# Sample pairs inside the attention, and an out-projection that begins while its last norm group is summed

## What is computed

```
z = rmsnorm(x) @ w_in                     # split among the three mixers
out_a = RG-LRU(z)                         # 256 wide
out_b = MLA(z)                            # 8 heads x 64 = 512 wide
out_c = GLA(z)                            # 4 heads x 64 = 256 wide, normed and gated
merged = concat(rmsnorm(out_a, n_a), rmsnorm(out_b, n_b), rmsnorm(out_c, n_c))
x = x + merged @ w_out                    # 1024 x 1024
x = x + hier_moe(rmsnorm(x))              # best of 4 groups, 2 of its 8 experts
```

## Time and profile before

| | before |
|---|---|
| median of 3 runs | 1611.6 us (1609.57 to 1612.38) |
| the profiled execution | 1611.4 us, its span 1609.5 us |
| mean granted TensorE clock | 0.888 of full speed |
| TensorE busy | 1275.7 us, 79% of the span |
| TensorE weight loads | 767.7 us, 48% |
| VectorE busy | 545.7 us, 34% |
| ScalarE busy | 359.1 us, 22% |
| GpSimd busy | 320.8 us, 20% |
| chain of waits, by engine | PE 52%, DMA 22%, DVE 11%, waits for nothing shown 6%, SyncE's queue 4% |

### The profile page before, as it was taken

One profiled execution on the slowest core, in us unless ns is written; L12 is line 12 of the kernel. 1 busy time (PEld: TensorE's weight loads), 2 busy tenths in 40 slices (PEclk: granted clock), 3 DMA queues, 4 the chain that ended last, 5 costly groups with the idle time before them and its releaser, 6 DMA issues.

```text
span 1609.5 us, 21838 instructions
## 1 busy us (share of the span) xinstructions
PE 1275.7 (79%) x7203; PEld 767.7 (48%) x7204; DVE 545.7 (34%) x1345; ACT 359.1 (22%) x823; POOL 320.8 (20%) x729
## 2 busy tenths in 40 slices
PE   5999977769956887778499997866898477888881
PEld 4777555434453443444277765533446244444440
DVE  2275685102243111111516557731113411111115
ACT  4233336121111101111314333522311011011112
POOL 0012410000002333333102052000000133333440
PEclk9999999669957999999699999975897599999996
DMA  5310021442094889995521002064207499978745
GB/s 211 99 36 27 9 80 45 165 144 78 40 385 168 344 348 400 408 407 227 197 97 63 27 0 88 1 205 136 92 13 286 175 381 408 377 275 344 292 174 182
DMA packets 98900, 299.11 MB, mean 186 GB/s; under 512 B 13230, under 2 KB 29966, under 8 KB 98450
## 3 DMA queue, kind: packets, MB, share of 16 engines
q1 hardware_dynamic: 85426, 273.21, 45.3%
q0 software_dynamic: 13408, 25.04, 4.3%
HBM read 289.96 MB, written 27.09 MB: 197 GB/s over the span
## 4 chain that ended last, share of the span: by engine, by line
PE 52%; DMA 22%; DVE 11%; issue 6%; SPq 4%; ACT 2%; POOL 2%; POOLq 1%; DVEq 0%; ACTq 0%
DMA ra<-h_rows,slot_now 19%; PE bank L1542 14%; PE bank L1818 9%; PE bank L1876 5%; PE bank L1887 3%; PE bank L1858 3%; SPq L495 2%; PE bank L1831 2%; PE bank L1574 2%; DVE rg L1262 1%; PE bank L1740 1%; PE bank L1662 1%; PE bank L1666 1%; PE bank L1807 1%; DVE rf L1259 1%
## 5 line engine op out<-in xcount | busy, mean ns | idle before, releaser
L1542 PE MATMUL bank<-ra,rb 128*128 128x288 f32 (+1 forms) x896 | 225.2, 414 | 1.9 <-ACT ra L736 1.9
L1542 PEld LDWEIGHTS bank<-ra,rb 128*128 128x128 f32 (+1 forms) x896 | 170.4, 191 | 54.0 <-issue 3.6
L1477 DVE COPY rb<-bank 128x512 f32<-128x512 f32 x71 | 49.1, 692 | 223.0 <-DMA y_rows<-rb,home_now 158.1
L990 ACT ACTIVATE rb<-bank 128x128 f32<-128x128 f32 x71 | 19.7, 278 | 417.9 <-PE bank L1876 417.9
L1858 PE MATMUL bank<-cst,ra 128*128 128x128 f32 x292 | 49.7, 295 | 74.3 <-DMA ra<-h_rows,slot_now 74.2
L1876 PE MATMUL bank<-rg,rb 128*64 128x256 f32 x768 | 92.3, 395 | 8.0 <-issue 5.2
L1887 PE MATMUL bank<-re,rb 128*64 128x512 f32 x296 | 81.5, 677 | 14.2 <-DVE rb L1473 14.2
L1471 DVE TENSOR_TENSOR rb<-rb,bank 128x128 f32<-128x128 f32 x71 | 20.4, 288 | 196.8 <-ACT rb L990 196.8
L1876 PE MATMUL bank<-re,rb 128*64 128x256 f32 x736 | 84.8, 383 | 2.5 <-issue 0.8
L697 POOL DMA_INDIRECT ra<-h_rows,slot_now x73 | 77.1, 1056 | 39.7 <-issue 39.7
L1876 PEld LDWEIGHTS bank<-rg,rb 128*64 128x64 f32 x768 | 56.7, 142 | 53.2 <-issue 29.2
(11 more groups left out here) (354 smaller groups left out, 2055.6 us busy)
## 6 DMA issues: line engine op xcount, KB each, us to landing
rg<-in_w_moe SPq DMA_DIRECT2D x24, 2048.0 KB, 11.3
re<-in_w_moe SPq DMA_DIRECT2D x20, 2048.0 KB, 13.0
re<-in_w_moe SPq DMA_DIRECT2D x30, 1024.0 KB, 15.0
rg<-in_cache SPq DMA_DIRECT2D x128, 192.0 KB, 3.5
rg<-in_w_moe SPq DMA_DIRECT2D x24, 1024.0 KB, 13.7
rf<-in_w_moe SPq DMA_DIRECT2D x10, 2048.0 KB, 12.4
ra<-in_w_moe SPq DMA_DIRECT2D x10, 2048.0 KB, 13.4
rb<-in_win SPq DMA_DIRECT2D x28, 512.0 KB, 3.8
```

What stands on the lines that cost most here:

```text
L1477: V.tensor_copy(ysb, bank[5][:, :]).then_inc(S["y_ready"], 1)
L1542: ins = mm(bk[:mrows, 0:HALF], win[:, n % 4, k, :mrows], hT[:, k, cols], start=k == 0, stop=k == KT - 1)
```

## The change

- **Sample pairs.** SAMPLE_AT puts the scores of the four pairs at steps 14, 19, 24 and 29, their values three steps and their turns six steps later; the loop gets a 36th step. The division of the probabilities is gone: VectorE scales the rows by the reciprocal while it copies them from PSUM (sample_rows, which was ScalarE's). ScalarE itself waits for the GLA state's output ahead of pair 0.
- **Pages.** Latents and transposes come by one load of 128 KB for each page, the keys by a second one of 16 KB, into rows 32p to 32p + 31 of a buffer of their own; the host lays them out as two inputs. To match, the rotary queries are turned into all 128 rows instead of 32. SyncE reads pair 0's page numbers ahead of its first wait, and both halves of the out-projection's weights stand behind all pages. Several buffers move; the first half of these weights goes where pages were.
- **Norm groups.** The slices are taken in MERGE_ORDER: RG-LRU, GLA, MLA. At steps 30 to 33 the first four are squared, summed, and scaled. The four of MLA follow behind the loop.
- **Out-projection.** For the first column half TensorE multiplies the first four slices of tiles 0 to 2 into three banks, then makes the MLA group's sums, then the first four slices of tiles 3 and 4, and then the last four of all five tiles. The second column half is as before.
- The first expert's weights are asked for when the fifth tile's result is there.

The core of the diff:

```diff
-ATT_STEPS = HEADS * 4 + 3
+ATT_STEPS = HEADS * 4 + 4
 STATE_STEPS = (0, 1, 2, 4, 6)
 INTER_STEP = STATE_STEPS[-1] + 1
 DP_STEPS = [INTER_STEP + 1 + d + d // 12 for d in range(CH)]
-SAMPLE_STEP = 27
-SAMPLE_ORDER = (("scores", 1), ("scores", 2), ("values", 1), ("values", 2), ("turn", 1), ("turn", 2),
-                ("scores", 3), ("values", 3), ("turn", 3))
+SAMPLE_AT = (14, 19, 24, 29)
+EARLY_STEP = 30
+MERGE_ORDER = (0, 1, 6, 7, 2, 3, 4, 5)
+NORM_GROUPS = {0: (0, 2, 256), 2: (2, 4, 256), 1: (4, 8, 512)}
...
-    if s == SAMPLE_STEP:
-        keys += [("ss", 0, k) for k in range(3)]
-    if s == SAMPLE_STEP + 3:
-        keys += [("sp", 0, k) for k in range(3)] + [("sv", 0)]
-    if s == SAMPLE_STEP + 6:
-        keys += [("svt", 0)]
+    for p, at in enumerate(SAMPLE_AT):
+        if s == at:
+            keys += [("ss", p, k) for k in range(3)]
+        if s == at + 3:
+            keys += [("sp", p, k) for k in range(3)] + [("sv", p)]
+        if s == at + 6:
+            keys += [("svt", p)]
...
-for kind, p in SAMPLE_ORDER:
-    keys += {"scores": [("ss", p, k) for k in range(3)],
-             "values": [("sp", p, k) for k in range(3)] + [("sv", p)], "turn": [("svt", p)]}[kind]
-keys += [("uvs",)]
-keys += [("osum", k, h) for k in range(3) for h in range(2)]
-keys += [("wo", n, t) for n in range(2) for t in range(TT)]
+    if s == EARLY_STEP + 1:
+        keys += [("osum", g, h) for g in (0, 2) for h in range(2)]
+keys += [("uvs",)] + [("wo", 0, t) for t in range(3)]
+keys += [("osum", 1, h) for h in range(2)]
+keys += [("wo", 0, t) for t in range(3, TT)] + [("wo", 1, t) for t in range(TT)]
...
-wout = [cut(rb, 0, KT, 512), cut(ra, 0, KT, 512)]
+wout = [cut(rg, 0, KT, 512), cut(ra, 0, KT, 512)]
...
-spread = cut(rb, 1152, SEQ)
+spread = cut(re, 13568, SEQ)
...
-pg = [cut(rg, 6144 * k, 2, NPAGE, 3 * P) for k in (1, 0)]
-CKV, CKVT, KPET = slice(0, P), slice(P, 2 * P), slice(2 * P, 3 * P)
-sprob = cut(re, 8960, 1088)
-spT = cut(re, 10048, 9, P)
-osq = cut(rg, 0, 8, T)
-ors = cut(rg, 4608, 3, T)
+pg = [cut(rg, 4096, 2, NPAGE, 2 * P), cut(rb, 0, 2, NPAGE, 2 * P)]
+kpg = cut(rg, 8192, 2, NPAGE, P)
+CKV, CKVT = slice(0, P), slice(P, 2 * P)
+sprob, sprob_new = cut(rg, 10240, 1024), cut(re, 2944, NS)
+spT, spT_new = cut(rg, 11264, 8, P), cut(re, 3008, P)
+osq = cut(rg, 4096, 8, T)
+ors = cut(re, 8960, 3, T)
...
-take(sp, L, ("inter", 2))
-sp.wait_ge(S["gla_out"], 32 * (L + 1))
 for p in range(4):
     page = [sp.value_load(pages[0:1, col:col + 1], min_val=0, max_val=a["cache"].shape[1] - 1)
             for col in range(2 * p * NPAGE, 2 * (p + 1) * NPAGE)]
-    if p == 1:
-        sp.wait_ge(S["out_c"], L + 1)
+    if p == 0:
+        take(sp, L, ("inter", 2))
+        sp.wait_ge(S["gla_out"], 32 * (L + 1))
     if p > 1:
         take(sp, L, ("sv", p - 2))
     for n in range(2 * NPAGE):
         sp.dma_start(pg[p % 2][:, n // NPAGE, n % NPAGE, :],
                      a["cache"][L, bass.ds(page[n], 1)].rearrange("a p n -> (a p) n")) \
             .then_inc(page_in[p % 2], 16)
-    if p == 2:
-        after(sp, L, ("pv", 3))
-        sp.dma_start(wout[0], wo_rows[:, :, 0:512]).then_inc(wout_in[0], 16)
-    if p == 3:
-        take(sp, L, ("pv", 3))
-        sp.dma_start(wout[1], wo_rows[:, :, 512:1024]).then_inc(wout_in[1], 16)
+        sp.dma_start(kpg[ROPE * p:ROPE * (p + 1), n // NPAGE, n % NPAGE, :],
+                     a["cache_kpe"][L, bass.ds(page[n], 1)].rearrange("a p n -> (a p) n")) \
+            .then_inc(kpage_in[p % 2], 16)
+sp.wait_ge(S["out_c"], L + 1)
+sp.dma_start(wout[0], wo_rows[:, :, 0:512]).then_inc(wout_in[0], 16)
+take(sp, L, ("pv", 3))
+sp.dma_start(wout[1], wo_rows[:, :, 512:1024]).then_inc(wout_in[1], 16)
...
-sp.wait_ge(S["merged"], 8 * (L + 1))
+take(sp, L, ("wo", 0, TT - 1))
...
-def sample_rows(p):
-    bk = take(act, L, ("sv", p))
-    give(copy(svs[:, p % 2, :], bk[:, 0:P]), ("sv", p))
...
+def squares(slots):
+    for n in slots:
+        fn(osq[:, n, :], merged[MERGE_ORDER[n]], ACT.Square).then_inc(S["osq_ready"], 1)
+def group_rstds(*groups):
+    rstds(L, *[(("osum", g, h), ors[:, g, cols], NORM_GROUPS[g][2], "ors_ready")
+               for g in groups for h, cols in enumerate(halves)])
...
-give(copy(qp[0:ROPE, :, :].rearrange("p b (h e q) -> p e h b q", e=2, q=NQ)[:, e],
-          bk[0:ROPE, 0:4 * NS].rearrange("p (h b q) -> p h b q", b=NB, q=NQ)), ("qp", e))
+give(copy(qp[:, :, :].rearrange("p b (h e q) -> p e h b q", e=2, q=NQ)[:, e],
+          bk[:, 0:4 * NS].rearrange("p (h b q) -> p h b q", b=NB, q=NQ)), ("qp", e))
...
-    if s == SAMPLE_STEP + 1:
-        sample_exp(0)
-    if s == SAMPLE_STEP + 3:
-        probabilities_out(0)
-    if s == SAMPLE_STEP + 4:
-        sample_rows(0)
-    if s == SAMPLE_STEP + 6:
-        sample_out(0)
-sample_exp(1)
-probabilities_out(1)
-sample_exp(2)
-sample_rows(1)
-probabilities_out(2)
-sample_rows(2)
-sample_out(1)
-sample_out(2)
-sample_exp(3)
-probabilities_out(3)
-sample_rows(3)
-sample_out(3)
+    for p, at in enumerate(SAMPLE_AT):
+        if s == at + 1:
+            if p == 0:
+                act.wait_ge(S["gla_out"], 32 * (L + 1))
+            sample_exp(p)
+        if s == at + 3:
+            probabilities_out(p)
+        if s == at + 6:
+            sample_out(p)
+    if s == EARLY_STEP:
+        act.wait_ge(S["out_c"], L + 1)
+        for p in range(3):
+            take(act, L, ("sv", p))
+        squares(range(0, 4))
+    if s == EARLY_STEP + 2:
+        group_rstds(0, 2)
 act.wait_ge(S["out_b"], L + 1)
 for p in range(4):
     after(act, L, ("pv", p))
-for k in range(8):
-    fn(osq[:, k, :], merged[k], ACT.Square).then_inc(S["osq_ready"], 1)
-rstds(L, *[(("osum", k, h), ors[:, k, cols], n, "ors_ready")
-           for k, n in enumerate((256, 512, 256)) for h, cols in enumerate(halves)])
+squares(range(4, 8))
+group_rstds(1)
...
-    link(V.reciprocal(sm[:, 89:90], sm[:, 88:89]))
-    V.tensor_scalar(sprob, sprob, sm[:, 89:90], None, ALU.mult).then_inc(S["s_prob"], 1)
+    V.reciprocal(sm[:, 89:90], sm[:, 88:89]).then_inc(S["s_sums"], 1)
+def sample_rows(p):
+    bk = take(dve, L, ("sv", p))
+    dve.wait_ge(S["s_sums"], 4 * L + p + 1)
+    give(V.tensor_scalar(svs[:, p % 2, :], bk[:, 0:P], sm[:, 89:90], None, ALU.mult), ("sv", p))
+def normed_groups(slots, ready):
+    dve.wait_ge(S["ors_ready"], 6 * L + ready)
+    for n in slots:
+        k, g = MERGE_ORDER[n], (0, 0, 2, 2, 1, 1, 1, 1)[n]
+        V.scalar_tensor_tensor(merged[k], merged[k], vec[:, V_ON + k:V_ON + k + 1], ors[:, g, :],
+                               ALU.mult, ALU.mult).then_inc(S["merged"], 1)
...
-if s == SAMPLE_STEP:
-    sample_max(0)
-if s == SAMPLE_STEP + 1:
-    sample_divide(0)
+for p, at in enumerate(SAMPLE_AT):
+    if s == at:
+        sample_max(p)
+    if s == at + 1:
+        sample_divide(p)
+    if s == at + 4:
+        sample_rows(p)
+if s == EARLY_STEP + 3:
+    normed_groups(range(0, 4), 4)
...
-for p in range(1, 4):
-    sample_max(p)
-    sample_divide(p)
...
-for k, g in enumerate((0, 0, 1, 1, 1, 1, 2, 2)):
-    if k in (0, 2, 6):
-        dve.wait_ge(S["ors_ready"], 6 * L + 2 * g + 2)
-    V.scalar_tensor_tensor(merged[k], merged[k], vec[:, V_ON + k:V_ON + k + 1], ors[:, g, :],
-                           ALU.mult, ALU.mult).then_inc(S["merged"], 1)
+normed_groups(range(4, 8), 6)
...
+pe.wait_ge(kpage_in[p % 2], 16 * 2 * NPAGE * (2 * L + p // 2 + 1))
+rows = slice(ROPE * p, ROPE * (p + 1))
...
-ins = mm(bk[64 * b2:64 * b2 + 64, 0:n], qp[0:32, 2 * p + b2, :],
-         pg[p % 2][0:32, b2, 4 * k:4 * k + 4, KPET] if k < 2 else kpeT[0:32, SEQ:T],
+ins = mm(bk[64 * b2:64 * b2 + 64, 0:n], qp[rows, 2 * p + b2, :],
+         kpg[rows, b2, 4 * k:4 * k + 4, :] if k < 2 else kpeT[rows, SEQ:T],
...
-pe.wait_ge(S["s_prob"], 4 * L + p + 1)
+for k in range(3):
+    after(pe, L, ("ss", p, k))
...
-ins = mm(bk[0:ROPE, n * NS:(n + 1) * NS], sel[rows, 0:ROPE], qt[rows, 2 * n + e, SEQ:T],
+ins = mm(bk[:, n * NS:(n + 1) * NS], sel[rows, :], qt[rows, 2 * n + e, SEQ:T],
...
+def group_sums(g):
+    n0, n1, _ = NORM_GROUPS[g]
+    pe.wait_ge(S["osq_ready"], 8 * L + n1)
+    for h, cols in enumerate(halves):
+        bk = begin(pe, L, ("osum", g, h))
+        for n in range(n0, n1):
+            ins = mm(bk[:, 0:HALF], ones, osq[:, n, cols], start=n == n0, stop=n == n1 - 1)
+        done(ins, ("osum", g, h))
...
-if s == SAMPLE_STEP:
-    for e in range(2):
-        after(pe, L, ("qa", e))
-        after(pe, L, ("qp", e))
-        after(pe, L, ("kr", e))
-    after(pe, L, ("ctok",))
-    sample_scores(0)
-if s == SAMPLE_STEP + 3:
-    sample_values(0)
-if s == SAMPLE_STEP + 6:
-    sample_turn(0)
+for p, at in enumerate(SAMPLE_AT):
+    if s == at:
+        for e in range(2):
+            after(pe, L, ("qa", e))
+            after(pe, L, ("qp", e))
+            after(pe, L, ("kr", e))
+        after(pe, L, ("ctok",))
+        sample_scores(p)
+    if s == at + 3:
+        sample_values(p)
+    if s == at + 6:
+        sample_turn(p)
...
```

(58 more changed lines are left out.)

11 lines of the change are left out of this document (2 added, 9 removed).

## The result

The changed kernel took 1552.8, 1551.2 and 1570.16 us, the first of them profiled (span 1551.0, clock 0.916). A fourth execution stood at 4292.87 us and is left out of the comparison, but not of the median of four, 1561.48. The ratio to the kernel before is 0.9668, 95% interval 0.9586 to 0.975. The forecast was 1550 (1516 to 1580): the direction and the time are right.

| stretch | before | after | forecast |
|---|---|---|---|
| scores of tile 14 to tile 27 | 38.5, 38.5 | 76.2, 76.1 | 65.7 |
| tile 27 to the first out-projection product | 108.9, 107.0 | 41.3, 41.3 | 45.9 |
| out-projection | 69.4, 71.1 | 73.6, 73.6 | 73.3 and 75.0 |
| sum | 216.8, 216.6 | 191.1, 191.0 | 184.9, 186.6 |

What follows compares the result with a forecast made beforehand. Bound: the serial chain of waits from attention to out-projection, mostly at half clock. Gains of 31.9 us in layer 0 and 30.0 in layer 1, less 0.8 for the query turn: 1611.4 - 61.1 = 1550.3, so 1550 (1516 to 1580).

Steps and rivals of the forecast that it cites:

- TensorE's work at nearly full clock: Tile 14 to 27: three score blocks, two value blocks and two turns add 23.3 us a layer at full clock.
- bank waits for the exponentials: Tile 14 to 27: TensorE waits 2.7 us a pair, 8.1 in all, until ScalarE's exponentials free the score banks.
- waits for the copies: Tile 14 to 27: value products wait for the copies of their transposes, 0.92 us each, 1.8 in all.
- old idle time that is filled: Tile 14 to 27: the new work fills TensorE's 6.0 us of idle time, which is subtracted.
- VectorE's copy of the rows: In the attention loop: VectorE's scaled copy of the value rows replaces ScalarE's 0.27 us copy, at no cost.
- 5.9 us of half clock: After tile 27: pair 2's products (1.9) and pair 3's scores (4.0) run at half clock, adding 5.9 us.
- The rest: Tile 27 to the out-projection without the half-clock addition: the order of waits adds up to 40.0 us.
- The second rival: From tile 27 all TensorE blocks run at half clock, 11.1 us a layer more: 1572 us; chance 0.16.
- the third group's sums: Inside the out-projection: these sums stand between its products, adding 3.9 us with no wait.
- the cover of 7 us: Out-projection: first halves hide copy, squares and signals (about 3.5 us), then logarithm, table load, exponentials, first normed slice (about 3.6).
- the query turn: The wider turn (128 columns for 32) costs TensorE 0.4 us a layer, bounds 0 and 0.9.
- third rival: SyncE's load issues become the bound: no gain at 0.85 us a load, 1673 us at 1.09; chance 0.04.

Runs made afterwards that it cites:

- early read: Against the changed kernel, VectorE copies a pair's value rows out of PSUM first in its step, not last: 1540.18 us, again 1537.06.
- the two later groups: The changed kernel run again unchanged, twice, as base beside variants: 1566.88 and 1559.37 us.
- the best version: Early read plus early sums between pair 3's transposes and products, pairs 1 to 3 and early squares one step earlier: 1521.29 us, 0.9452 of the kernel before.

## Why the prediction was right, and where it was not

The direction and most of the gain were right because the mechanism was: the chain behind the attention (waits on pages, pair behind pair, cold clock) was replaced by TensorE's own work in the loop. That 1552.8 came within 3 us of 1550 is luck: a layer took 10.5 us more than forecast up to tile 27 and 4.6 less behind it, so that the stages gave 10.6 us too little, and 7.3 us outside them made up for most of that. Tile 14 to tile 27, in us a layer:

| term | forecast | measured | from |
|---|---|---|---|
| TensorE's work at nearly full clock | 23.3 | 21.0 | early read, layer 1 (clock 0.97): 53.51 less 32.55 |
| bank waits for the exponentials | 8.1 | 5.6 | 2.19, 1.66, and 1.76 before tile 26 |
| waits for the copies | 1.8 | 3.6 | 1.94, 1.62 |
| old idle time that is filled | -6.0 | -4.7 | the rest of 15.46 |
| VectorE's copy of the rows | 0 | 5.0 | 3.39, 1.58 |
| clock | 0 | 7.2 | 60.69 less 53.51 |
| sum over 38.5 | 27.2 | 37.7 | 76.15 less 38.53 (37.6) |

The fourth row is what is left of the idle time, so the column adds up by construction. Layer 0 of the early read divides the busy time otherwise: 23.8 us of work and 4.3 of clock.

- The step that failed is one sentence: "VectorE's scaled copy replaces ScalarE's 0.27 copy: nothing." The copy itself costs nothing (0.35). But its place, last in VectorE's step, puts a PSUM read behind the whole step's other work, and with eight banks going round that holds TensorE. The bank waits had been worked out for the exponentials alone. Moved first, it gives back 10.1 us in layer 1 and 7.6 in layer 0. That this leaves 65.9 in layer 1, beside the forecast's 65.7, is chance in its turn: it has less work and more idle time than the forecast, and layer 0 is at 68.6.
- The clock was looked for in the wrong place. From tile 27 the prediction put 5.9 us of half clock; pair 3's scores ran at full clock, and only pair 2's products (3.30 for 1.97) and the early sums (5.84 for 3.88) did not, 3.3 in all. Timeline and chain of waits of the changed kernel:

```profile
307.40 3.30 PE L1703 MATMUL bank<-rg 128*64 128x128 f32 x32 [4.50 <-ACT re L888]
```

```profile
322.76 5.84 PE bank L1743 x16
```

  The rest was 38.0, not 40.0: 41.3 for 45.9. The wait ahead of pair 2's products is 4.50, where 3.7 had been worked out. Before tile 27 it allowed for none, and there it cost 7.2. The second rival ("the loop stays cold") came true in part, in a stretch that it did not name.
- Right to the tenth: the third group's sums inside the out-projection (3.88 for 3.9), and no wait behind them. Of the cover of 7 us the first part is real: with the sums ahead of the out-projection they wait 3.14 us (3.5 had been worked out), and another 3.2 go to the clock. The second part, 3.6, did not open in that run and is not shown.
- Within its bounds (0 and 0.9): the query turn. Its sixteen products take 1.60 us instead of 0.89, and the steps up to tile 14 0.7 us more a layer, where 0.4 had been taken. The new key rows show no price: pair 3's score products, on rows 96 to 127, take 1.07 us each four, as pair 0's.
- Right: SyncE has room, and more than forecast. Pair 3's last load was issued at 291.0 and its scores came at 312.7. One load more per page crossed the third rival's threshold.
- By the Trainium skill (ScalarE: Activation LUTs, section What ACT_TABLE_LOAD costs) each switch of tables would cost a drain too. In the rows above the operation behind each load starts 0.01 us after it: no drain, as forecast by the row.
- What made 1552.8 out of 1560 is the gain outside, most of it within chance. The medians of the two later groups are 1566.9, with a layer 0 that the clock made 10 us longer, and 1559.4.

## What to carry to other kernels

When the reader of a PSUM bank moves to another engine, ask not what the read costs but where it stands in that engine's order, and who takes that bank next. Work that moves into a loop also brings short waits into it, and on TensorE they can be paid twice, in the wait and in the clock: here 3 us of waiting cost 10 in one layer and 8 in the other. The early half of the sum paid here only where something filled the time in which the other half was normed; without the open banks it gave nothing that the runs can tell.

## What the runs showed of the hardware

Two kernels that differ in the place of one read, with the same last three waits to 0.01 us, ran the 17 us behind them at a granted clock of 0.50 and of 0.90; the second had 1.9 us less waiting ahead of those. In one trace of the changed kernel layer 0 spent 9.2 us more of TensorE's busy time on the same instructions than layer 1. The changed kernel's executions lie 0.15, 0.95 and 1.2% apart in its three groups, with group medians up to 0.9% apart; the best version's lie 0.2% apart in its one group.
